# First block of a two-block transformer kernel: constants issued by GpSimd, value tiles in pairs, meta rows in one bank, projection in the experts' banks

## The reference, cut to what matters

```python
def token_mix(a, w_in, lb, rec_norm_w, lq1, lk1, lq2, lk2, subln_w, w_out, lam_init, cos, sin):
    proj = jnp.einsum('btd,dc->btc', a, w_in)
    aq, ak, av, rq, rf, ri, rg = jnp.split(proj, SPLIT_POINTS, axis=-1)
    att = diff_attention(aq, ak, av, lq1, lk1, lq2, lk2, subln_w, lam_init, cos, sin)
    rec = hgrn2(rq, rf, ri, rg, lb, rec_norm_w)
    mixed = jnp.concatenate([att, rec.astype(att.dtype)], axis=-1)
    return jnp.einsum('btc,cd->btd', mixed, w_out)
...
        a = rmsnorm(h, mix_norm_w[l])
        h = h + token_mix(a, w_in[l], lb_all[l], rec_norm_w[l], ...)
        h = h[:, N_META:]
        h = h + peer_ffn(rmsnorm(h, ffn_norm_w[l]), peer_w_query[l], peer_subkeys[l],
                         peer_u[l], peer_v[l]).astype(h.dtype)
    return rmsnorm(h, final_norm_w)
```

## Time and profile before

| | us |
|---|---|
| median of 3 runs | 2019.4 |
| lowest and highest run | 2016.98, 2019.96 |
| profiled execution, first to last instruction (its span) | 2014.6 |
| PE, DVE, ACT, POOL busy in it | 1671.1, 1328.1, 658.9, 589.6 |
| software queue (gathers), share of 16 DMA engines | 65.4% |
| hardware queue (SP's), share | 26.6% |

### The profile page before, as it was taken

How to read it: one execution, slowest core, us unless ns; L and a number is a source line. 1 busy time by engine, 2 the same in 40 slices (tenths; PEclk the granted TensorE clock), 3 DMA queues, 4 the chain that set the end, 5 groups by cost and what they waited for, 6 DMA issues and landing times.

```text
span 2014.6 us, 20417 instructions
## 1 busy us (share of the span) xinstructions
PE 1671.1 (83%) x6878; PEld 830.8 (41%) x6878; DVE 1328.1 (66%) x3461; ACT 658.9 (33%) x1239; POOL 589.6 (29%) x516
## 2 busy tenths in 40 slices
PE   7977798678898998786589988899996877877997
PEld 7436463225454443233145434443434322222653
DVE  4227787975788888876876678966665579744231
ACT  3122433323344265221241134521221245311361
POOL 0002333432332343434433323333223334321000
PEclk9988998989999998888889999899998998899999
DMA  6438999999999998999999999999999999999665
GB/s 225 123 117 333 416 417 418 420 418 416 398 394 354 354 413 340 371 418 417 422 418 418 418 404 369 387 419 418 418 413 351 417 410 402 420 417 374 194 220 192
DMA packets 132903, 738.52 MB, mean 367 GB/s; under 512 B 15920, under 2 KB 17584, under 8 KB 67264
## 3 DMA queue, kind: packets, MB, share of 16 engines
q0 software_dynamic: 73728, 536.90, 65.4%
q1 hardware_dynamic: 59072, 200.32, 26.6%
HBM read 735.07 MB, written 2.10 MB: 366 GB/s over the span
## 4 chain that ended last, share of the span: by engine, by line
PE 41%; DMA 27%; DVE 19%; issue 5%; ACT 5%; POOL 2%; SPq 0%; DVEq 0%; POOLq 0%; ACTq 0%
PE pa L844 22%; DMA uv_rows<-in_peer_uv,small 18%; PE py L844 10%; DMA wbuf<-in_wt 9%; PE pb L844 8%; DVE uv_rows L1809 6%; ACT area L1204 2%; ACT L1198 2%; POOL uv_rows L1999 2%; DVE tk L1819 1%; DVE tk L1818 1%; DVE area L1873 1%; ACT small L1204 1%; DVE small L1796 1%; ACT an L1204 1%
## 5 line engine op out<-in xcount | busy, mean ns | idle before, releaser
L1999 POOL DMA_INDIRECT uv_rows<-in_peer_uv,small x512 | 589.4, 1151 | 1245.9 <-PE py L844 984.7
L1809 DVE CUSTOM_DVE_ANT_0 uv_rows<-uv_rows,xrep 128x1024 f32<-128x1024 f32 x512 | 615.0, 1223 | 235.0 <-DMA uv_rows<-in_peer_uv,small 231.9
L844 PE MATMUL py<-uv_rows,tk 128*64 128x512 f32 x2048 | 563.5, 677 | 212.5 <-DVE tk L1819 209.3
L844 PE MATMUL pa<-wbuf,area 128*128 128x512 f32 (+1 forms) x800 | 374.7, 609 | 25.2 <-DMA wbuf<-in_wt 22.8
L1204 ACT ACTIVATE small<-small 128x2 f32<-128x2 f32 (+4 forms) x324 | 69.2, 214 | 861.4 <-DVE small L1809 831.5
L844 PEld LDWEIGHTS py<-uv_rows,tk 128*64 128x64 f32 x2048 | 135.9, 149 | 511.7 <-DVE tk L1819 282.6
L1198 ACT ACT_TABLE_LOAD x250 | 320.8, 1283 | 5.4 <-DVE small L1905 1.0
L844 PEld LDWEIGHTS pa<-wbuf,area 128*128 128x128 f32 (+1 forms) x800 | 141.3, 188 | 242.2 <-issue 197.7
L844 PE MATMUL pa<-area,wbuf 128*128 128x128 f32 (+2 forms) x1152 | 188.4, 322 | 22.7 <-issue 11.9
L844 PEld LDWEIGHTS pa<-area,wbuf 128*128 128x128 f32 x1152 | 166.2, 198 | 60.6 <-issue 34.3
L844 PE MATMUL pb<-wbuf,area 128*128 128x512 f32 x352 | 165.5, 616 | 14.6 <-DMA wbuf<-in_wt 9.6
(11 more groups left out here) (210 smaller groups left out, 1092.2 us busy)
## 6 DMA issues: line engine op xcount, KB each, us to landing
wbuf<-in_wt SPq DMA_DIRECT2D x352, 512.0 KB
uv_rows<-in_peer_uv,small POOLq DMA_INDIRECT x512
wbuf<-in_skT SPq DMA_DIRECT2D x15, 256.0 KB
h<-in_x SPq DMA_DIRECT2D x4, 512.0 KB
out<-h SPq DMA_DIRECT2D x4, 512.0 KB, 5.6
an<-in_x SPq DMA_DIRECT2D x3, 512.0 KB
area<-in_finw SPq DMA_DIRECT2D x2, 512.0 KB, 8.0
area<-in_masks SPq DMA_DIRECT2D x1, 512.0 KB, 6.8
```

What stands on the lines that cost most here:

```text
L844: return nc.tensor.matmul(o, l, r, start=start, stop=stop, skip_group_check=True)
L1809: last = V.tensor_tensor_reduce(uv_rows[:, n % RING, 0:D], uv_rows[:, n % RING, 0:D], xrep[:, b % 2, n % TG, :], 1.0, 0.0, ALU.mult, ALU.a ...
L1999: nc.gpsimd.indirect_dma_start(uv_rows[:, n % RING, :], None, t["peer_uv"], bass.IndirectOffsetOnAxis(ap=expert_ids[:, c:c + 1].bitcast(U3 ...
```

## The change

Four things are changed, for block 0 alone. GpSimd issues the twelve small constants and the masks, as soon as x has landed, where SP issued them between weight tiles. The tiles of `ri` and `av` are taken in pairs, ri[i] with av[i]: three banks are open through four pairs, and the 16 meta rows of both are collected in the third bank, ri's in its rows 0 to 15 and av's in rows 32 to 47. The output gate `rg` moves from behind the third head's scores to the place where `av` was, behind the first head's. The projection collects in the two `py` banks, its recurrent half (tiles 2 and 3) first, each column half at its own place between the heads' steps, its attention half (tiles 0 and 1) after `a3`; DVE adds each to `h1` and signals `out_added`, on which the norm ahead of the experts and the first experts' sum wait.

```diff
+    def both(i):
+        return [ri[i], av[i]]
+
+    def out(c, *parts):
+        return [("out", g, c, i) for i in parts]
...
-    rows += [aq[0:1], [("ly", b, 1)], aq[1:3], [("lx", b, 2), ("lm", b, 1)], aq[3:4], ri[0:1], [("ly", b, 2), ("rotq", g)]]
-    rows += [ri[1:2], [("lx", b, 3), ("lm", b, 2)], ri[2:3], [("ly", b, 3), ("kd", b)], ri[3:4], [("lm", b, 3), ("ke", b)]]
-    rows += [us(0), av, [("uw", b, 0)], [("ut", b, 0)], us(1), [("kdt", b), ("uw", b, 1), ("st", b)]]
-    rows += [[("uv", b, 0), ("ut", b, 1)], us(2), rg, [("r1", b), ("uw", b, 2)], [("uv", b, 1), ("ut", b, 2)], us(3)]
-    rows += [[("r2", b), ("uw", b, 3), ("r3", b)], [("uv", b, 2), ("ut", b, 3)], [("uv", b, 3)], [("a1", b), ("a2", b), ("a3", b)]]
-    return rows + [tiles("out", g, 0) + tiles("out", g, 1)]
+    rows += [aq[0:1], [("ly", b, 1)], aq[1:3], [("lx", b, 2), ("lm", b, 1)], aq[3:4], both(0), [("ly", b, 2), ("rotq", g)]]
+    rows += [both(1), [("lx", b, 3), ("lm", b, 2)], both(2), [("ly", b, 3), ("kd", b)], both(3), [("lm", b, 3), ("ke", b)]]
+    rows += [us(0), rg, [("uw", b, 0)], [("ut", b, 0)], us(1), [("kdt", b), ("uv", b, 0), ("uw", b, 1), ("st", b)]]
+    rows += [[("ut", b, 1)], us(2), [("r1", b), ("uv", b, 1), ("uw", b, 2), ("r2", b)], [("ut", b, 2)], us(3)]
+    rows += [[("r3", b), ("uv", b, 2), ("uw", b, 3)], out(0, 2, 3), [("ut", b, 3)], [("uv", b, 3)], out(1, 2, 3)]
+    return rows + [[("a1", b), ("a2", b), ("a3", b)], out(0, 0, 1), out(1, 0, 1)]
...
+    if g == (0,) and name in ("ri", "av", "out"):
+        return (3 if name == "av" and i == 3 else 0), 0, 1
...
+        def mixed_in(b):
+
+            return (b_free, B_AT[("out", GROUP_OF[b], 1, 3)]) if b else (out_added, 2)
...
                 if s == ("rf", (0,), 3):
-                    for name, dst in CONSTS:
-                        sp.dma_start(dst, t[name]).then_inc(ld_c, 16)
                     load_angles((0,))
-                elif s == ("rq", (0,), 3):
-                    sp.dma_start(masks.bitcast(I32), t["masks"]).then_inc(ld_k, 16)
...
+            def first_rows(name, i):
+
+                if name == "ri":
+                    if i == 0:
+                        open_banks.extend(a_bank() for _ in range(3))
+                    first_tile[:] = [cut(tile(), 2, W)]
+                else:
+                    first_tile.append(cut(tile(), 2, W))
+                src, meta = inputs_of((0,)), open_banks[2]
+                n = int(name == "av")
+                for k in range(2):
+                    last = mm(open_banks[n][:, :], src[:, 2 * i + k, 0:P], first_tile[n][:, k, :], i + k == 0, i == 3 and k == 1)
+                if i == 3:
+                    last.then_inc(a_full, 1)
+                if n:
+                    for k in range(2):
+                        rows_ = [mm(meta[32 * m:32 * m + NM, :], src[:, 2 * i + k, P:], first_tile[m][:, k, :],
+                                    i + k == 0, i == 3 and k == 1) for m in range(2)]
+                    rows_[0].then_inc(w_done, 1)
+                    rows_[1].then_inc(*((a_full, 1) if i == 3 else (w_done, 1)))
+                    if i == 3:
+                        open_banks.clear()
+
+            def first_out(c, i):
+
+                w = cut(tile(), 2, W)
+                for k in range(2):
+                    last = mm(psum_y[c][:, :], inputs_of((0,))[:, 2 * i + k, 0:P], w[:, k, :], i == 2 and k == 0, i == 1 and k == 1)
+                last.then_inc(w_done, 1)
...
-                    pe.wait_ge(b_free, B_AT[("out", GROUP_OF[b], 1, 3)])
+                    pe.wait_ge(*mixed_in(b))
...
+                elif name == "out" and s[1] == (0,):
+                    c, i = s[2:]
+                    if c == 0 and i % 2 == 0:
+                        pe.wait_ge(b_free, B_AT[("r3" if i else "a3", 0)])
+                    first_out(c, i)
...
+            def take_first_rows():
+                empty(rec_v[:, 0, :], bank()[:, :])
+                empty(v[:, 0, :], bank()[:, :])
+                ps = bank()
+                fn(rec_v_meta, ps[0:NM, :], ACT.Copy)
+                empty(v[0:NM, 4, :], ps[32:32 + NM, :])
...
-                act.wait_ge(b_free, B_AT[("out", GROUP_OF[b], 1, 3)])
+                act.wait_ge(*mixed_in(b))
...
+                elif name == "out" and s[1] == (0,):
+                    c = s[2]
+                    if s[3] == 1:
+                        if c == 0:
+                            dve.wait_ge(ld_h, 16)
+                        dve.wait_ge(w_done, FREED[LOADS.index(s)][1])
+                        half = h1[:, 0, W * c:W * (c + 1)]
+                        V.tensor_tensor(half, half, psum_y[c][:, :], ALU.add).then_inc(out_added, 1)
...
         def _(pool):
+            pool.wait_ge(ld_x[0], 16)
+            for name, dst in CONSTS:
+                pool.dma_start(dst, t[name]).then_inc(ld_c, 16)
+            pool.dma_start(masks.bitcast(I32), t["masks"]).then_inc(ld_k, 16)
```

More of the change, by code:

```diff
@@ L274, in use @@
         return 1, 0, 1
+    if g == (0,) and name in ("ri", "av", "out"):
+        return (3 if name == "av" and i == 3 else 0), 0, 1
     if name in ROWS_IN or name in ROWS_2 or name in ("ga", "gb"):
-        return ((nb + (meta if name in ("av", "ri") else 0)) if i == 3 else 0), 0, 1
+        return (nb if i == 3 else 0), 0, 1
     if name in ("out", "wo"):
@@ L668, in build @@
         y_ready = sem("y_ready")
+        out_added = sem("out_added")
         rf_done, fin_ready, stored = sem("rf_done"), sem("fin_ready"), sem("stored")
@@ L786, in _ @@
                         load_angles(GROUP_OF[s[1]])
-                elif s[0] == "out" and s[2:] == (0, 0):
+                elif s[0] == "out" and s[2:] == ((0, 0) if s[1][0] else (0, 2)):
                     for b in s[1]:
@@ L820, in _ @@
             na, nb, nw, rows = [0], [0], [0], [0]
-            open_banks = []
+            open_banks, first_tile = [], []
             def a_bank():
@@ L851, in cols_tile, with rows_tile @@
                 last.then_inc(a_full, 1)
-            def rows_tile(src, g, i, n_tiles, bank, full, meta=False, k0=0):
+            def rows_tile(src, g, i, n_tiles, bank, full, k0=0):
                 w = cut(tile(), 2, W)
@@ L857, in rows_tile @@
                     open_banks.clear()
-                    open_banks.extend(bank() for _ in range(len(g) + meta))
+                    open_banks.extend(bank() for _ in range(len(g)))
                 for j, ps in enumerate(open_banks):
                     for k in range(2):
-                        if j < len(g):
-                            last = mm(ps[:, :], src[:, k0 + 2 * i + k, P * j:P * (j + 1)], w[:, k, :],
-                                      i + k == 0, i == n_tiles - 1 and k == 1)
-                        else:
-                            last = mm(ps[0:NM, :], src[:, k0 + 2 * i + k, P * len(g):], w[:, k, :], i + k == 0, i == n_tiles - 1 and k == 1)
+                        last = mm(ps[:, :], src[:, k0 + 2 * i + k, P * j:P * (j + 1)], w[:, k, :],
+                                  i + k == 0, i == n_tiles - 1 and k == 1)
                     if i == n_tiles - 1:
@@ L1099, in _ @@
                     g, i = s[1:]
-                    rows_tile(inputs_of(g), g, i, 4, a_bank, a_full, meta=g == (0,) and name != "rg")
+                    if g == (0,) and name != "rg":
+                        first_rows(name, i)
+                    else:
+                        rows_tile(inputs_of(g), g, i, 4, a_bank, a_full)
                 elif name == "lm":
@@ L1259, in take_rows @@
                     empty(dst, bank()[:, :], ACT.Silu if name == "rg" else ACT.Copy)
-                if g == (0,) and name != "rg":
-                    empty(rec_v_meta if name == "ri" else v[0:NM, 4, :], bank()[0:NM, :])
             def forget_gates(g):
@@ L1397, in _ @@
                     take_cols(*s)
-                elif name in ROWS_IN and s[2] == 3:
+                elif name == "av" and s[1:] == ((0,), 3):
+                    take_first_rows()
+                elif name in ROWS_IN and s[2] == 3 and (s[1] != (0,) or name == "rg"):
                     take_rows(s[0], s[1])
```

## The result

The changed kernel takes 1999.01 us (median of 4 runs, 1996.3 to 2001.27) against 2019.43 before (4 runs, 2016.98 to 2019.96): ratio 0.9911, 95% interval 0.989 to 0.9932, so 14 to 22 us less. 2000.4 was forecast, in a range from 1997.0 to 2008.5, and faster by more than 0.2%, which it is. The profiled execution took 1998.28 us with a span of 1996.5, 18.1 under the span before. Span and run differ by only 1.8 here, so 3.0 of the 4.8 that I added to come to the median were scatter: other runs of the kernel before reach from 2012.2 to 2021.9, and the medians of its sets from 2016.0 to 2019.4.

What follows compares the result with a forecast made beforehand. A 168.5 us opening, mostly bound by PE, precedes a 1846 us loop paced by its gathers. Terms -5.2 - 4.4 - 9.4 = -19.0 us give a span of 1995.6, median 2000.4 with 4.8 added; range 1997 to 2008.5.

Steps and rivals of the forecast that it cites:

- Part 1: Opening up to the second head's scores: ri and av tiles paired, gate tiles moved to av's place; -5.2 us.
- The rival without overlap: Meta products of a pair don't run side by side: 1.7 us more per pair, 7 in all, 2007.4; chance 0.09.
- neighbouring products: Pairs' meta products: neighbours in different columns overlap, as in the experts' products, so four cost 1.72 us plus 0.18.
- Part 2: Second head's scores to last weighted values: gate tiles leave, first half of recurrent projection enters; -4.4 us.
- The net of -0.9: Heads' stretch: PE's 2.3 us wait for DVE against the table load leaving and 1.3 us of clock regained.
- Part 3: Projection: other recurrent half runs during the ACT and DVE tail, leaving eight attention products and one add; -9.4 us.
- Part 4: Start of the opening: GpSimd issues constants and masks, landing in time by 1 to 2 us; 0 us.
- a gain of 1.1: Constants: PE's 1.10 us wait for ak's tile may go, against a possible 1.3 us later rq tile.
- Late loads: Landings take 7 us, not 4.9; pairs 2 and 3 and projection wait 1 to 2 us each: 2003 to 2006; chance 0.07.
- Given back in the loop: The earlier start only finds a full DMA queue draining at the same time: 2010 to 2019; chance 0.06.
- Constants holding everything: Forget gates wait for constants issued by GpSimd at over 3.2 us each; about 2025 at 3.5; chance 0.03.
- the sign of trouble: Opening: the prediction counted as wrong if ACT's exponential of lambda moved beyond 30 us.

Runs made afterwards that it cites:

- e5: Changed kernel with av's meta products in the first experts' bank, in the same array columns as ri's; ratio to the kernel before 0.9942.
- e2: Changed kernel with a pair's four meta products reordered, ri's two then av's two instead of in turn; ratio to the kernel before 0.9917.
- e7: Changed kernel with lambda and lower bound steps ahead of the forget gate's tiles, the three pair banks opened one by one; ratio to the kernel before 0.9912.
- e6: Changed kernel with two unused 128x512 products where PE waits for the third head's weights; ratio to the kernel before 0.989.
- e4: Changed kernel with the output gate's four tiles back behind the third head's scores; ratio to the kernel before 0.9936.
- e3: Changed kernel with the whole projection after a3, still in the experts' banks, no recurrent half ahead; ratio to the kernel before 0.9941.
- e1: Kernel before with only GpSimd issuing the twelve constants and the masks; ratio to the kernel before 0.9994.
- e9: e8 without filler at the start, with the gate's log earlier on ACT and filler in the state step; ratio to the kernel before 0.9871.
- e8: e6 and e7 together, plus filler products before the first transposes and during the norm of the experts' input; ratio to the kernel before 0.9875.

## Why the prediction was right, point by point

*Where the time is.* The reading of the profile held: an opening, then a loop that starts with the first expert numbers and keeps its length. The eleven profiles show this over 27 us of first gathers. That the median came within 1.4 us of 2000.4 is luck in part: the opening gave 15.7 us of the 19.0, and the median fell by 20.4, since the set of runs before lay high (2019.4, where other sets have 2016.0 and 2017.6) and the loop varies by several us. The total can't tell 15.7 from 19.0, both being within 14 to 22; the stretches can.

*Part 1, pairs (-5.2 forecast, -3.8 measured).* The price of a pair was right, 5.43 us measured against 5.3, and e5 shows that two column groups give the 1.7 us each that I put on them. The rival without overlap, whose price was 7 us, is closed by e5: that is what it would have cost (6.84). The reason that I had taken for it, neighbouring products, was too narrow (e2). The difference of 1.4 has three sources: 0.1 a pair; 0.57 us of waiting for ACT because all three banks are opened at once, which I had not priced (e7 takes it away); and aq starting 0.26 us later.

*Part 2, the heads (-4.4 forecast, -1.9 measured).* This is the term that was mis-sized. I named the gap and its cause (2.3 us forecast, 2.15 measured) but left only 0.9 us for the half clock behind it (2.2 less the 1.3 got back). PE ran at 0.50 for 7.6 us at least (104.4 to 112.0), over the fourth head's scores, the transposes and the first projection lot, which I had put at 3.5 and which took 5.05. e6 gives 3.5 us back in that stretch by filling the gap, more than the whole shortfall of 2.5. Taking the sum of squares later on DVE, which would be the other way to close the gap, wasn't tried. A further 0.8 was lost in the state step, which took 5.28 us with the products behind it against 4.50 before, and no run shows why. (The net of -0.9 in the forecast also needs 1.9 us for the table load that leaves, a size that it doesn't state.) The move of the gate's tiles by itself is worth about 3 us (e4), and without the first lot this stretch is 5.9 shorter (e3). My reading that the clock is low after each idle place was too simple: e1 has the full clock behind a wait of 1.87 us.

*Part 3, the projection (-9.4 forecast, -9.7 measured).* Right in size, and the cause is shown by e3: with the half back behind a3 this stretch, D, is 9.3 longer. Together with what the first lot costs in part 2, taking the half ahead is worth 3.4 us net.

*Part 4, the constants (0 forecast).* Right in the sum, not in the way. GpSimd issues a plain transfer every 0.53 to 0.72 us, not every 1.24 as with gathers, and starts at 5.46, so the masks go out at 12.12 and no longer come between rq and ak. The 1.10 us for ak's tile went, and DVE's decay inputs were late in its place (e1). I had given a gain of 1.1 as a bound without asking what is late next. The rule on descriptors built by GpSimd's cores (the Trainium skill, "SBUF — State Buffer", section "SBUF: two separate sides") wasn't put to a test: the issues kept their pace while DVE was busy for 3.38 us of the 7.3 from 5.4 to 12.7, and whether its steps there are of the kind that the rule means no run here tells.

*Rivals.* Late loads: PE's rows from 52 to 87 have no wait for a tile. Given back in the loop: no, by the table. Constants holding everything: no; the masks, the last of them, landed near 16.6 us, and ACT's exponential of lambda came at 28.57, where more than 30 was the sign of trouble. The first gather and the add to h both came 3.3 us later than the forecast had them.

## What to carry to other kernels

Price an idle place of PE at what stands behind it too: the 2.15 us gap here cost another 3.5 us through the clock behind it, and two products without use in the gap took that back. Such a price is not certain in every execution (e1), and it can be due behind waits of under 1 us (e4). When a wait is taken away, find the next late input at the same place of the queue before counting the gain: in e1 a wait for DVE took the place of the one for the tile, and in e7 DVE had to wait for ACT. Products of few rows can share the array if they are put in different columns, as the two of 16 rows at 0 and 32 here. And read the effect of an edit from its own stretches rather than from the end of the opening: e3's 5.2 us were 3.4.

## What the runs showed of the hardware that was not expected

Products for two column groups (16 columns at 0 and at 32) overlap in both orders tried: four products take 1.9 us in turn and 1.9 us one group after the other, 3.44 in the same columns (e5). The granted clock of one and the same stretch differs from profile to profile: the state step's 16 records took 2.05 us (e6), 1.95 (e9, with filler ahead), 3.08 (before), 3.4 to 3.6 (e1, e3, e7), 3.78 (the changed kernel, e2, e4, e5 and e8). The two waits of PE ahead of it are the same, 0.9 and 0.8 us, in e6, where it was fast, and in the changed kernel, e2, e3, e5, e7 and e8, where it was slow. What decides between them I can't say. A plain transfer costs GpSimd about half of what a gather does to issue.
